# Modulation columns in the bank of their own products, and the group sums of the next step freed of waiting for them

## The chip, the cores and the metric
The kernel runs on one core of one Trainium2 chip. The metric is device time in microseconds (us) of one execution, the median of several runs. Before the change it is 2300.29 us (three runs, 2299.01 to 2300.86).

## What is computed
The reference is a two-layer backbone over 256 context and 256 latent tokens of width 1024. Layer 0 mixes tokens with a bidirectional Mamba-2 (SSD) mixer and then has a dense SwiGLU; layer 1 has windowed attention and a top-2-of-8 mixture of experts. Each layer is modulated by six vectors made of the condition. The change touches layer 0's mixer and its modulation alone. Cut to these, the reference is:

```python
mod_x = (silu(c) @ w_mod[i] + b_mod[i]).reshape(-1, 6, D_MODEL)        # and mod_c from c_ctx
hx = modulate(rmsnorm(x, norm1_w[i]), mod_x[:, 0], mod_x[:, 1])
...
def gated_rmsnorm(y, z, w):                                            # end of the SSD mixer
    g = (y * silu(z)).reshape(shp[:-1] + (SSD_GROUPS, D_INNER // SSD_GROUPS))
    g = g * rsqrt(mean(g * g, axis=-1, keepdims=True) + EPS)           # a mean over each group
    return g.reshape(shp) * w
...
out = gated_rmsnorm(y, z, norm_w) @ w_out
x = x + mod_x[:, 2][:, None] * yx
```

The mean square over each of the 8 groups (256 channels) is what "group sums", "group root", "group inverse" and "group spread" make below. The modulation vectors of layer 0 are made in 12 pairs of 512 columns; the first four are needed at once, the other eight (parts 2 to 5) only after the mixer, and they are made in the gaps of the group loop.

## The kernel before
**Layout.** Activations lie with channels on the partitions and the 512 tokens along the row. Weights come as units of 128 x 2048 numbers into a ring of four buffers; of each, ScalarE makes a high part (`dense_high`, L1211) and VectorE the rest (`dense_low`, L1608), and TensorE forms each product from three matmuls (`thrice`, L645, lines L647 to L649). Every engine's program is written out by hand, in the order in which it runs, and the engines wait for one another's semaphores with constants. The eight PSUM banks are `ps[0]` to `ps[7]`.

**The group loop.** TensorE's loop (L811) runs over g = 0 to 6; ScalarE's (L1366) and VectorE's (L1847) run alongside. In this document "pass g" is one turn of it. In pass g TensorE

1. at the head, if g > 0, makes the sums of group g-1 (`group_sums`, L698: 16 small matmuls into `ps[4]`, line L704);
2. does half of the x projection of group g+1 (24 matmuls of 512 columns, into `ps[0]` and `ps[1]`), then, if g > 0, `group_spread` (L708: 8 matmuls into `ps[5]`, line L713), which broadcasts the reciprocal roots, then the other half;
3. turns group g's tiles to tokens (`to_tokens`, L716: lines L723, L730 and L736, the last into `ps[5]`);
4. does the "bc" projection of group g+1, into `ps[0]` and `ps[1]` again, after it has waited for ScalarE's evacuation of x (`gemm_evac`, L820), with the chunk states (L744) in its middle;
5. makes one pair of modulation rows (`mod_pair`, L615, 32 matmuls of line L622, into `ps[5]`), the group's outputs (L766) and the z projection;
6. turns the modulation rows into columns (`turn_pair`, L626, 8 matmuls of line L631, into `ps[4]`), after VectorE has copied the rows out of `ps[5]` (`mod_rows`, L1640, line L1644).

VectorE, in pass g: the addition of bias to the columns of the pass before (`mod_out`, L1646, line L1655, which reads `ps[4]`), the reciprocal of the roots (`group_inverse`, L1748), a rest part, `finish` (L1757, which reads the spread), the token scales (`token_scales`, L1770), the decay tiles and the states, `mod_rows`, a rest part, one convolution (8 operations of L1742), the gating, a rest part and the second convolution. So `mod_out` stands behind the second convolution of the pass before. ScalarE, in pass g: z's evacuation (L1256), two Silus of the convolution (L1270), `group_root` (L1275, which reads the sums), a high part (L1219), 32 exponentials of segments (L1287), x's evacuation (L1248), the token tiles (L1297) and so on. Table loads stand between Silu, square root and exponential.

After the loop the last two groups follow, among the first parts of the output projection (`out_part`, L675), whose banks are 0 to 5.

Of the kernel before, what the change touches and what calls it, by code (L numbers as in the profile page):

```python
# [284 lines left out]
def backbone(nc, xt_in, vecs, wdt_in, bv_in, dense, experts_w, consts, out):  # L285
    es = ExitStack()
    with es:
# [7 lines left out]
        def sb(name, n, dt=F32):  # L295
            nonlocal top
            place_of[name] = top
            top += 4 * (n + (-n) % 8)
            assert top <= SB_BASE + 4 * SB_WORDS, (name, top)
            return at(name, place_of[name], n, dt)  # L300
# [13 lines left out]
        modT = sb("modT", 192)[:].rearrange("p (l m r) -> p l m r", l=2, m=48)  # L314
# [140 lines left out]
        ps = [es.enter_context(nc.psum_tensor(f"ps{i}", [P, 512], F32)) for i in range(8)]  # L455
# [14 lines left out]
        def vc(row, n=1):  # L470
            return col[:, row:row + n] if isinstance(row, int) else col[:, bass.ds(row, n)]


        S = {}
# [120 lines left out]
        def _(pe):  # L595
# [19 lines left out]
            def mod_pair(p, bank):  # L615

                for i in range(2):
                    n = D_AT[("m0", MOD_PAIRS[p][i], 0)]
                    pe.wait_ge(d_in[D_SLOT[n]], D_ARRIVED[n])
                    for k in range(KT):  # L620
                        c0 = 32 * (k % 4)
                        last = mm(ps[bank][c0:c0 + 32, 256 * i:256 * i + 256], csT[:, k, :],  # L622
                                  d_raw[D_SLOT[n]][:, 256 * k:256 * k + 256], start=k < 4, stop=k >= 4)
                    last.then_inc(S["d_used"], 1)

            def turn_pair(p, bank):  # L626

                pe.wait_ge(S["mrow_sb"], p + 1)
                for t in range(4):
                    a = 512 * (p % 2) + t * P  # L630
                    last = mm(ps[bank][:, 2 * t:2 * t + 2], mrow[:, a:a + P], rowsel, start=True, stop=True)  # L631
                last.then_inc(S["modt_ps"], 1)
# [42 lines left out]
            def out_part(j, h, ks):  # L675

                n = D_AT[("wout", j, h)]
                dense_wait(n)
                for k in ks:
                    pe.wait_ge(S["glo_done"], 1 + next(c for c, (a, w) in enumerate(G_CHUNKS) if a <= k < a + w))  # L680
                    top, low, _ = gate_parts(k, 1)
                    for t in range(2):
                        last = thrice(ps[OUT_BANK[2 * j + t]][:], dense_tile(n, k - 8 * h, t), (top, low), k == 0, k == 15)
                return last

            def gemm_part(kind, g, banks, ks):

                n = D_AT[(kind, g, 0)]
                dense_wait(n)
                for k in ks:  # L690
                    if g == 0:
                        pe.wait_ge(S["n_low"], k + 1)
                    for t in range(2):
                        last = thrice(ps[banks[t]][:], dense_tile(n, k, t), (h_top[:, k, :], h_low_[:, k, :]),
                                      k == 0, k == KT - 1)
                return last

            def group_sums(g):  # L698

                pe.wait_ge(S["ysq_done"], 2 * g + 2)  # L700
                pe.wait_ge(S["mod_done"], 5 + g)
                for t in range(2):
                    for c in range(NCH):
                        last = mm(ps[4][32 * c:32 * c + 32, 0:P], ones[:, 0:32], ysq[:, t, c * P:c * P + P],  # L704
                                  start=t == 0, stop=t == 1)
                last.then_inc(S["gsum_done"], 1)

            def group_spread(g):  # L708

                pe.wait_ge(S["grinv_done"], g + 1)  # L710
                for c in range(NCH):
                    pick = ident[:, 32 * c:32 * c + 1].to_broadcast([P, P])
                    last = mm(ps[5][:, c * P:c * P + P], pick, grs, start=True, stop=True)  # L713
                last.then_inc(S["gspread"], 1)

            def to_tokens(g):  # L716

                pe.wait_ge(S["cx_ready"], 4 * g + 4)
                pe.wait_ge(S["gemm_evac"], 6 * g + 6)
                for ch in range(NCH):  # L720
                    for t in range(2):
                        o = (ch % 2) * 256 + t * P
                        last = pe.transpose(ps[2 + ch // 2][:, o:o + P], cx[:, t, ch * P:ch * P + P], ident)  # L723
                    if ch % 2:
                        last.then_inc(S["tr_ready"], 1)
                if g == 0:
                    pe.wait_ge(S["ac_exp"], 1)
                    pe.wait_ge(S["ac_tail"], 1)
                for ch in range(NCH):
                    last = pe.transpose(ps[4][:, ch * P:ch * P + P], cx[:, 2, ch * P:ch * P + P], ident)  # L730
                last.then_inc(S["tr_ready"], 1)
                if g:
                    pe.wait_ge(S["gT_done"], 2 * g)
                for ch in range(NCH):
                    s = slice(ch * P, ch * P + P)
                    last = mm(ps[5][:, s], cx[:, 2, s], cx[:, 3, s], start=True, stop=True)  # L736
                last.then_inc(S["tr_ready"], 1)

            def states(g):

                pe.wait_ge(S["tok_evac"], 4 * g + 3)
                pe.wait_ge(S["xs_ready"], 2 * g + 2)
                for n, (d, ch) in enumerate(((0, 0), (0, 1), (0, 2), (1, 1), (1, 0), (1, 3))):
                    last = mm(ps[2 + n // 2][:, (n % 2) * 256:(n % 2) * 256 + 256], btok[:, ch, :], xtl[d][:, ch, :],  # L744
                              start=True, stop=True)
                last.then_inc(S["st_ready"], 1)
# [64 lines left out]
            for g in range(7):  # L811
                if g:
                    group_sums(g - 1)
                pe.wait_ge(S["gemm_evac"], 6 * g + 4)
                gemm_part("x", g + 1, (0, 1), range(4))
                if g:
                    group_spread(g - 1)
                gemm_part("x", g + 1, (0, 1), range(4, KT)).then_inc(S["d_used"], 1)
                to_tokens(g)
                pe.wait_ge(S["gemm_evac"], 6 * g + 8)  # L820
                gemm_part("bc", g + 1, (0, 1), range(4))
                states(g)
                gemm_part("bc", g + 1, (0, 1), range(4, KT)).then_inc(S["d_used"], 1)
                pe.wait_ge(S["tok_evac"], 4 * g + 4)
                mod_pair(4 + g, 5)
                if g == 0:
                    pe.wait_ge(S["ac_rows_sb"], 1)
                outputs(g)
                gemm_part("z", g + 1, (2, 3), range(KT)).then_inc(S["d_used"], 1)
                turn_pair(4 + g, 4)  # L830

            group_sums(6)
            group_spread(6)
            to_tokens(7)
            pe.wait_ge(S["gemm_evac"], 6 * 7 + 4)
# [1 line left out]
            states(7)  # L837
            pe.wait_ge(S["tok_evac"], 32)
            mod_pair(11, 5)
            pe.wait_ge(S["st_op"], 80)  # L840
            turn_pair(11, 4)
            out_part(1, 0, range(8)).then_inc(S["d_used"], 1)
            outputs(7)
            out_part(0, 1, range(8, 14))
            group_sums(7)
            out_part(1, 1, range(8, 14))
            group_spread(7)
# [733 lines left out]
        def _(dv):  # L1581
            TS, TT, STT = dv.tensor_scalar, dv.tensor_tensor, dv.scalar_tensor_tensor
# [63 lines left out]
            def mod_out(p):  # L1646

                dv.wait_ge(S["modt_ps"], p + 1)
                if p < 4:
                    dst = modT[:, 0, 0:16, :].rearrange("p (s k) r -> p s k r", s=2)[:, :, 2 * p:2 * p + 2, :]  # L1650
                    bias = vc(V_BMOD, 16).rearrange("p (s k) -> p s k", s=2)[:, :, 2 * p:2 * p + 2]
                    TT(dst, ps[3 + p % 2][:, 0:8].rearrange("p (s k r) -> p s k r", s=2, k=2),
                       bias.unsqueeze(3).to_broadcast([P, 2, 2, 2]), ALU.add).then_inc(S["mod_done"], 1)
                else:
                    TT(modT[:, 0, 4 * p:4 * p + 4, :], ps[4][:, 0:8].rearrange("p (m r) -> p m r", m=4),  # L1655
                       vc(V_BMOD + 4 * p, 4).unsqueeze(2).to_broadcast([P, 4, 2]), ALU.add).then_inc(S["mod_done"], 1)

            def first_alpha(p):
# [16 lines left out]
            for q in range(2):  # L1675
                r = slice(64 * q, 64 * q + 64)
# [366 lines left out]
            r = 0  # L2043
# [153 lines left out]
```

## Time and profile before

| | before |
|---|---|
| median of three runs | 2300.29 us (2299.01 to 2300.86) |
| the profiled execution's own time | 2299.07 us |
| its span, first to last instruction | 2297.3 us |
| mean granted TensorE clock | 0.964 |
| TensorE matmul busy | 2161.5 us |
| VectorE busy | 1495.1 us |
| ScalarE busy | 1236.9 us |
| bytes read from HBM | 504.45 MB, 221 GB/s over the span |

The span is what the profile's positions count in; the execution's own time is 1.8 us longer. The group loop lies between about 100 and 453 us of the span; the experts take the second half, in which the DMA engines are busy by 90% or more. A busy share is an average over stages with different limits. In the rows of time below, a number in brackets is the idle time of that engine before the instruction, and behind the arrow is what ended it; "PE" is TensorE, "DVE" VectorE, "ACT" ScalarE.

### The profile page before, as it was taken

The page shows a single profiled execution, that of the slowest core. Times are in us where ns is not written, and L with a number is a line of the kernel's source. Part 1 is how long each engine was busy: PE and PEld are TensorE (multiplying, and loading weights), DVE is VectorE, ACT ScalarE, POOL GpSimd, SP SyncE. Part 2 cuts the span into 40 slices and gives each one's busy share as a digit, 9 for nine tenths or more (in the row PEclk, how much of TensorE's full clock was granted, in tenths as well). Part 3 has the DMA queues.
Part 4 walks back from the last instruction along what each step waited for, and adds up shares of the span by engine and source line. Part 5 has one row for each costly group of instructions (what it writes and reads, how often), then busy time and mean ns, then how long its engine had stood idle before and what let it go on. Part 6 is the DMA issues. An engine that isn't in the chain of part 4 may idle for free.

```text
span 2297.3 us, 27395 instructions
## 1 busy us (share of the span) xinstructions
PE 2161.5 (94%) x11224; PEld 1729.8 (75%) x11224; DVE 1495.1 (65%) x1479; ACT 1236.9 (54%) x1394; POOL 45.7 (2%) x20
## 2 busy tenths in 40 slices
PE   6799999989899999988987999999999999999997
PEld 4678777767677777867566787887878787888875
DVE  3467777653332322245856887888878887888874
ACT  4566666642322222143545766676766666676763
POOL 0011111100000000000000000000000000000000
PEclk9899999979899999989997999999999999999998
DMA  8233454422244444325105999999999999999990
GB/s 301 94 129 129 148 185 173 173 94 74 87 170 165 166 169 155 107 74 175 48 1 193 345 344 356 330 364 334 342 340 342 339 338 350 336 362 333 344 344 21
DMA packets 137733, 509.61 MB, mean 222 GB/s; under 512 B 15296, under 2 KB 15680, under 8 KB 135296
## 3 DMA queue, kind: packets, MB, share of 16 engines
q1 hardware_dynamic: 137520, 507.65, 62.0%
q8 instruction: 90, 1.47, 0.3%
q14 instruction: 43, 0.35, 0.0%
q10 hardware_dynamic: 80, 0.13, 0.0%
HBM read 504.45 MB, written 3.28 MB: 221 GB/s over the span
## 4 chain that ended last, share of the span: by engine, by line
PE 83%; DVE 7%; ACT 4%; issue 1%; DVEq 0%; ACTq 0%
PE ps L1048 14%; PE ps L1046 14%; PE ps L1047 13%; PE ps L647 10%; PE ps L649 10%; PE ps L648 10%; DVE area L1742 3%; DVE d_lo L1613 2%; PE ps L957 1%; PE ps L975 1%; PE ps L1032 1%; PE ps L1105 1%; ACT area L1287 1%; PE ps L1075 1%; PE ps L659 1%
## 5 line engine op out<-in xcount | busy, mean ns | idle before, releaser
L2039 DVE TENSOR_TENSOR w_lo<-w_raw,w_hi 128x2048 fp32r<-128x2048 f32 x336 | 749.4, 2286 | 51.6 <-ACT w_hi L1496 50.7
L1496 ACT ACTIVATE w_hi<-w_raw 128x2048 fp32r<-128x2048 f32 x336 | 625.9, 1918 | 78.9 <-PE ps L1048 77.8
L1613 DVE TENSOR_TENSOR d_lo<-d_raw,d_hi 128x2048 fp32r<-128x2048 f32 (+1 forms) x76 | 171.9, 2262 | 334.4 <-ACT d_hi L1219 334.4
L1046 PE MATMUL ps<-w_hi,x_hi 128*128 128x512 f32 x896 | 357.1, 399 | 2.0 <-DVE x_lo L2095 2.0
L647 PE MATMUL ps<-h_top,d_hi 128*128 128x512 f32 (+1 forms) x816 | 331.5, 406 | 25.2 <-DVE h_low L1605 9.8
L1048 PE MATMUL ps<-w_hi,x_lo 128*128 128x512 f32 x896 | 355.0, 396 | 0.0
L1047 PE MATMUL ps<-w_lo,x_hi 128*128 128x512 f32 x896 | 350.7, 391 | 0.0
L1219 ACT ACTIVATE d_hi<-d_raw 128x2048 fp32r<-128x2048 f32 (+1 forms) x76 | 143.7, 1890 | 382.8 <-DMA d_raw<-in_dense 245.2
L649 PE MATMUL ps<-h_top,d_lo 128*128 128x512 f32 (+1 forms) x816 | 322.9, 396 | 0.0
L648 PE MATMUL ps<-h_low,d_hi 128*128 128x512 f32 (+1 forms) x816 | 319.1, 391 | 0.0
L647 PEld LDWEIGHTS ps<-h_top,d_hi 128*128 128x128 f32 x816 | 158.3, 194 | 69.6 <-issue 26.2
L1048 PEld LDWEIGHTS ps<-w_hi,x_lo 128*128 128x128 f32 x896 | 167.8, 187 | 41.6
L1047 PEld LDWEIGHTS ps<-w_lo,x_hi 128*128 128x128 f32 x896 | 168.5, 188 | 40.2
L1046 PEld LDWEIGHTS ps<-w_hi,x_hi 128*128 128x128 f32 x896 | 168.0, 187 | 39.2 <-DVE x_lo L2095 2.2
L649 PEld LDWEIGHTS ps<-h_top,d_lo 128*128 128x128 f32 x816 | 158.1, 194 | 35.7
L648 PEld LDWEIGHTS ps<-h_low,d_hi 128*128 128x128 f32 x816 | 158.9, 195 | 33.6
L1046 PE MATMUL ps<-w_hi,h_hi 128*128 128x512 f32 x448 | 179.9, 402 | 1.4 <-DVE h_lo L2111 1.4
L1048 PE MATMUL ps<-w_hi,h_lo 128*128 128x512 f32 x448 | 177.4, 396 | 0.0
L1047 PE MATMUL ps<-w_lo,h_hi 128*128 128x512 f32 x448 | 175.4, 392 | 0.0
L1048 PEld LDWEIGHTS ps<-w_hi,h_lo 128*128 128x128 f32 x448 | 83.9, 187 | 20.8
L1047 PEld LDWEIGHTS ps<-w_lo,h_hi 128*128 128x128 f32 x448 | 84.2, 188 | 19.9
L1046 PEld LDWEIGHTS ps<-w_hi,h_hi 128*128 128x128 f32 x448 | 84.0, 188 | 20.0 <-DVE h_lo L2111 1.7
(266 smaller groups left out, 2571.9 us busy)
## 6 DMA issues: line engine op xcount, KB each, us to landing
w_raw<-in_experts SPq DMA_DIRECT2D x672, 512.0 KB, 5.7
d_raw<-in_dense SPq DMA_DIRECT2D x240, 512.0 KB, 5.3
area<-acum_rows SPq DMA_DIRECT2D x16, 1024.0 KB, 8.4
d_raw<-in_dense SPq DMA_DIRECT2D x8, 384.0 KB, 4.2
xT<-in_xt SPq DMA_DIRECT2D x4, 512.0 KB, 6.7
gate_rows<-area SPq DMA_DIRECT2D x4, 512.0 KB, 6.7
hT<-gate_rows SPq DMA_DIRECT2D x2, 1024.0 KB, 6.0
cst<-in_consts SPq DMA_DIRECT2D x2, 512.0 KB, 11.2
```

The lines of the kernel that those rows point to most:

```text
L647: mm(o, w[0], v[0], start=first, stop=False)
L648: mm(o, w[0], v[1], start=False, stop=False)
L649: return mm(o, w[1], v[0], start=False, stop=last)
L659: last = mm(ps[6][c0:c0 + 32, 0:256], csT[:, k, :], d_raw[D_SLOT[n]][:, 256 * k:256 * k + 256], start=k < 4, stop=k >= 4)
L1046: mm(o, hi, w_hi[u % HIGH][:, a:a + 512], start=first, stop=False)
L1047: mm(o, hi, w_lo[u % RAW][:, a:a + 512], start=False, stop=False)
L1048: return mm(o, lo, w_hi[u % HIGH][:, a:a + 512], start=False, stop=last)
L1219: A(d_hi[si % D_HIGH][:, 0:w], d_raw[u][:, 0:w], ACT.Copy).then_inc(S["dhi_done"], 1)
L1496: A(w_hi[n % HIGH][:], w_raw[n % RAW][:], ACT.Copy).then_inc(S["whi_done"], 1)
L1613: TT(d_lo[u][:, 0:w], d_raw[u][:, 0:w], d_hi[si % D_HIGH][:, 0:w].bitcast(F32), ALU.subtract)\
L1742: STT(dst, raw[:, t, :, k:k + 256], vc(V_CW + 32 * k + conv_row(g, t)), dst, ALU.mult, ALU.add)\
L2039: TT(w_lo[n % RAW][:], w_raw[n % RAW][:], w_hi[n % HIGH][:].bitcast(F32), ALU.subtract)\
```

## The change
The turned columns of modulation pairs 4 to 11 are written into `ps[5]`, the bank in which their rows were made, and no longer into `ps[4]`; `mod_out` reads them there. `group_sums`, which writes `ps[4]`, no longer waits for `mod_out` (`mod_done`); `group_spread`, which writes `ps[5]`, now does, beside its wait for the reciprocal. The last turn loses its wait for the state operations of group 7 (`st_op`), which read `ps[4]`.

```diff
             def group_sums(g):
 
                 pe.wait_ge(S["ysq_done"], 2 * g + 2)
-                pe.wait_ge(S["mod_done"], 5 + g)
                 for t in range(2):
...
             def group_spread(g):
 
                 pe.wait_ge(S["grinv_done"], g + 1)
+                pe.wait_ge(S["mod_done"], 5 + g)
                 for c in range(NCH):
...
                 gemm_part("z", g + 1, (2, 3), range(KT)).then_inc(S["d_used"], 1)
-                turn_pair(4 + g, 4)
+                turn_pair(4 + g, 5)
...
             mod_pair(11, 5)
-            pe.wait_ge(S["st_op"], 80)
-            turn_pair(11, 4)
+            turn_pair(11, 5)
...
                 else:
-                    TT(modT[:, 0, 4 * p:4 * p + 4, :], ps[4][:, 0:8].rearrange("p (m r) -> p m r", m=4),
+                    TT(modT[:, 0, 4 * p:4 * p + 4, :], ps[5][:, 0:8].rearrange("p (m r) -> p m r", m=4),
                        vc(V_BMOD + 4 * p, 4).unsqueeze(2).to_broadcast([P, 4, 2]), ALU.add).then_inc(S["mod_done"], 1)
```

## Rows read from the trace of the kernel before

**Rows 1.** The page: busy time of the engines, and the chain that ended last.
```profile
PE 2161.5 (94%) x11224; PEld 1729.8 (75%) x11224; DVE 1495.1 (65%) x1479; ACT 1236.9 (54%) x1394; POOL 45.7 (2%) x20
...
PE 83%; DVE 7%; ACT 4%; issue 1%; DVEq 0%; ACTq 0%
```

**Rows 2.** Waits, 135 to 560 us: total us, times, longest us.
```profile
PE ps L704 <- DVE modT L1655: 9.2, 7, 1.5
...
PE ps L647 <- ACT area L1248: 1.3, 2, 0.7
```

**Rows 3.** Timeline, head of pass 2: start us, us, engine, line, operation.
```profile
200.60 0.95 PE L631 MATMUL ps<-cst 128*128 128x2 f32 x8
...
202.72 0.16 DVE L1655 TENSOR_TENSOR modT<-ps,col 128x8 f32<-128x8 f32 x1
...
203.02 0.65 PE L704 MATMUL ps<-area,cst 128*32 128x128 f32 x16 [1.47 <-DVE modT L1655]
...
205.18 0.95 DVE L1748 RECIPROCAL area<-area 128x128 f32<-128x128 f32 x1 [2.30 <-ACT area L1275]
...
210.82 1.05 PE L713 MATMUL ps<-area,cst 128*128 128x128 f32 x8
```

**Rows 4.** Timeline of ScalarE, pass 2.
```profile
202.17 1.29 ACT L1270 ACTIVATE area<-area 128x512 f32<-128x512 f32 x2 [0.29 <-DVE area L1742]
...
208.26 9.48 ACT L1287 ACTIVATE area<-area,atk 128x128 f32<-128x128 f32 x32
217.65 1.05 ACT L1248 ACTIVATE area<-ps 128x512 f32<-128x512 f32 x2
```

**Rows 5.** Timeline of VectorE, pass 2.
```profile
219.69 2.36 DVE L1770 TENSOR_TENSOR area<-area,tail 128x1024 f32<-128x1024 f32 x2 [6.37 <-ACT area L1297]
...
248.01 5.38 DVE L1742 SCALAR_TENSOR_TENSOR area<-area,col 128x512 f32<-128x512 f32 x8
```

**Rows 6.** Chain of waits in order of time: pass 1 (L1248) and pass 2 (L713).
```profile
167.78 0.97 ACT area L1248 x2
...
210.98 0.89 PE ps L713 x8
```

**Rows 7.** Timeline of VectorE: the copy of the modulation rows, passes 1, 2, 3, 5, 6.
```profile
184.71 0.69 DVE L1644 COPY cst<-ps 128x512 f32<-128x512 f32 x1 [0.18 <-PE ps L622]
...
235.30 0.69 DVE L1644 COPY cst<-ps 128x512 f32<-128x512 f32 x1 [0.81 <-PE ps L622]
...
285.92 0.69 DVE L1644 COPY cst<-ps 128x512 f32<-128x512 f32 x1 [0.84 <-PE ps L622]
...
386.40 0.69 DVE L1644 COPY cst<-ps 128x512 f32<-128x512 f32 x1 [0.73 <-PE ps L622]
...
437.01 0.69 DVE L1644 COPY cst<-ps 128x512 f32<-128x512 f32 x1 [0.83 <-PE ps L622]
```

**Rows 8.** Timeline of TensorE: first "bc" matmul of pass 1; last L736 of pass 2.
```profile
168.79 0.49 PE L647 MATMUL ps<-h_top,d_hi 128*128 128x512 f32 x1 [0.67 <-ACT area L1248]
...
218.59 1.06 PE L736 MATMUL ps<-area 128*128 128x128 f32 x8
```

**Rows 9.** Stretches: length, PE busy (count), granted clock, DMA share, GB/s.
```profile
168.80:172.20 3.40, 3.40 (x15) 1.00 0.44 175
203.67:210.80 7.13, 7.13 (x24) 0.76 0.21 82
304.88:310.40 5.52, 5.52 (x24) 1.00 0.27 106
...
355.28:361.90 6.62, 6.62 (x24) 0.83 0.17 71
```

**Rows 10.** Timeline of ScalarE behind the loop: the evacuation of the last z.
```profile
453.10 1.09 ACT L1256 ACTIVATE area<-ps 128x512 f32<-128x512 f32 x2 [4.83 <-PE ps L649]
```

**Rows 11.** Stretches in the router's part: transposes (L1011), and what follows them.
```profile
1227.95:1231.30 3.35, 3.35 (x18) 0.50 0.02 10
1231.40:1234.70 3.30, 0.99 (x9) 1.00 0.00 0
```

## The prediction
> **What bounds the kernel now.** I began with the shares on the page [rows 1]: TensorE is busy 94% of the span and carries 83% of the chain that ended last. That invites "every TensorE stall removed is time gained", but it is an average over stages, so I went on to the stage that is touched, the loop over the groups, some 400 us of 2297. I count by passes of that loop, 0 to 6; the sums of a group stand at the head of the pass after its own.
>
> The waits come next [rows 2]: `group_sums` (L704) sat 9.2 us in seven places for the addition that makes the modulation columns (L1655, VectorE): 1.5 us at the head of each of passes 1 to 6, and the little that is left behind the loop. In time order, at the head of pass 2 [rows 3]: the turning matmuls (L631) end at 200.60 + 0.95 = 201.55; the addition starts only at 202.72, because VectorE's queue holds a convolution ahead of it; TensorE idles 1.47 and starts the sums at 203.02. The group's reciprocal ends at 205.18 + 0.95 = 206.13, and the spread, which needs it, comes only at 210.82.
>
> Then the other engines, for what happens once TensorE is early. ScalarE [rows 4]: after the convolution's last Silu (202.17 + 1.29 = 203.46) it has no gap up to 218.70: square root, a high part, 9.48 us of segment exponentials from 208.26, and then the evacuation of the x projection (L1248, 217.65 to 218.70). The "bc" matmuls of TensorE write the same banks and wait for that evacuation. Behind it ScalarE reads the token tiles, for which VectorE had waited 6.37 us (L1770, 219.69) [rows 5]. From there VectorE is full up to the end of the pass's last convolution, 248.01 + 5.38 = 253.39, but for one hole: 0.81 us ahead of the copy of the modulation rows (L1644, in rows 7), which waits for the `mod_pair` matmuls behind "bc".
>
> So two loops of nearly one length run round each pass: one through VectorE and ScalarE (token scales, convolution, segments, evacuation), and TensorE's own. The chain of waits shows them change places [rows 6]: in passes 1 and 4 it runs through the evacuation L1248, in the others through TensorE's spread (L713). The hole ahead of L1644 tells the same [rows 7]: 0.18 us in pass 1 (and alike in pass 4), where the evacuation sets the pace; 0.81, 0.84, 0.73 and 0.83 in passes 2, 3, 5 and 6, where TensorE does. And where the evacuation does, TensorE waits for it already: 0.67 us at 168.79, the first "bc" matmul of pass 1 [rows 8].
>
> **The change, part by part.**
> 1. `group_sums` no longer waits for the addition. In pass 2 it may start at 201.6 instead of 203.0; its other condition, the squares, is met before ScalarE evacuates z. TensorE gains 1.5 us at this place, six times.
> 2. The wait moves to `group_spread`. The sums then end near 202.3, the 24 matmuls between take 5.5 us at the full clock [rows 9], so the spread is reached near 207.8. The addition is done at 202.9 and the reciprocal at 206.13: margins 4.9 and 1.7 us. The square root does not come earlier, as it stands behind the Silu that ends at 203.46. Cost 0, hidden by those 24 matmuls; without them the wait would stand here whole (behind the loop sums and spread follow each other, and nothing is gained).
> 3. The turn writes bank 5 instead of 4 and the addition reads it there: same instructions, same shapes, 0. The bank is free, since the turn already waits for its only reader, the copy L1644.
> 4. `turn_pair(11)` loses its wait for the state operations. VectorE copies the rows that it turns after those operations anyway: 0. No DMA moves and no queue's order changes, so SP's and POOL's queues stay as they are.
> 5. What is late next. In pass 2 the last small matmuls ahead of "bc" (L736) end at 218.59 + 1.06 = 219.65 [rows 8], after the evacuation's 218.70. Now they end near 218.2, so "bc" starts near 218.75, not 219.4: 0.65 us gained, and the other 0.8 turns into a wait. The hole ahead of L1644 falls from 0.81 to the 0.18 of the passes where the evacuation leads. In passes 1 and 4 nothing is gained: the wait of 0.67 grows to 2.15.
>
> The bounds of part 5: 0 if the freed time is lost entirely, 9.2 if all of it passes on. I take the value by the holes, which are the slack itself: (0.81 - 0.18) + (0.84 - 0.18) + (0.73 - 0.18) + (0.83 - 0.18) = 2.5 us. The last of the four passes on through the z matmuls, for which ScalarE waits 4.83 us at 453.10 [rows 10]. Everything after hangs on the loop's end and shifts as a whole.
>
> **The clock** is the unknown. After the sums of pass 2 the granted clock was 0.76 in the mean and the 24 matmuls took 7.13 us; in pass 5 they were 0.83 and 6.62; after those of pass 4, behind the same 1.5 us wait, 1.00 and 5.52 [rows 9]. A drop to 1.2 GHz costs 7.13 - 5.52 = 1.6 us, and now falls where part of it is slack. The change takes the wait from there and puts some 2.1 us ahead of "bc", behind transposes and small matmuls; a drop there delays L1644 and is paid whole. Bounds per pass: 0 and 1.6. I take 0, since behind the 0.67 us wait in the same place the clock stayed at 1.00 [rows 9], and keep 1.6 for the range: the new wait is three times as long.
>
> What transposes do for the clock decides here. From 1227.95 to 1231.30 TensorE did almost nothing but transposes, at 0.50, and right behind them the clock was 1.00 [rows 11]. The Trainium skill ("TensorE: Matmul & The Clock Gate", Part 4: PE-mode transpose) says that a transpose does not count as TensorE activity in the way other matmuls do. By that rule "bc" would start at the low clock in every pass, the result of rival C; the trace speaks against the rule.
>
> **Sum.** The profiled execution took 2299.07; 2299.07 - 2.5 = 2296.6. The median of the runs is 1.2 higher, 2300.29, and in its terms the forecast is **2297.8**. About 0.2% (4.6 us) is what a measurement can tell from no change.
>
> **Rivals.**
> A, the stall passes on whole: 2300.29 - 9.2 = 2291.1. For it: TensorE's 94% and its share of the chain. Against it: ScalarE's queue without a gap, and the 0.67 that TensorE waits already. It would need an earlier evacuation, and nothing brings that.
> B, the gain is given back: the low clock falls on "bc" in one or two of six passes, 1.6 each, which cancels 2.5: about 2300.3; three give 2302.6. For it: the clock fell in passes whose wait was 1.5 us. Against it: rows 11, and the 1.00 behind 168.79.
> C, slower: the low clock falls on "bc" in all six passes, as each has 2.1 us of waiting behind its transposes: 6 x 1.6 - 2.5 = +7.1, 2307.4. It passes 0.2% from five passes on (8.0 - 2.5 = 5.5). The same rows speak against it, more strongly, as every pass must fall.
> D, the change does not do what it says: the spread takes the wait over, no gain, 2300.3. For it only the thin margin of 1.7 us in part 2.
>
> **How the numbers follow.** Forecast 0.59, A 0.07, B 0.20, C 0.07, D 0.07. The range reaches up to three low-clock passes, 2302.6, and down to the forecast less the scatter of the runs (2299.01 to 2300.86) and a little of A, 2295.0; the rest of A and C are left out. Faster by over 0.2% is A and a little of the forecast, 0.09; slower is C, 0.07; within is the rest, 0.84.
>
> **What would show it.** Right: L704 waits for nothing, and neither does L713 in the loop; TensorE waits some 2.1 us for L1248 in all six passes; the hole before L1644 is 0.2 us everywhere; the chain runs through L1248 in each pass. Wrong by A: TensorE's waits for L1248 stay near 0.7. Wrong by B or C: a granted clock of 0.50 in the first "bc" matmuls, and holes before L1644 near 1.8. Wrong by D: waits at L713 of over 1 us. Holes gone and the time still lower than 2295 would show that I took a loop for closed that isn't.

## The result, and the profile after

The changed kernel takes **2305.74 us** (median of 9 runs, 2304.67 to 2307.52), against 2300.29 for the kernel before in the same comparison (9 runs, 2298.52 to 2301.93). The ratio is 1.0025, 95% interval 1.0016 to 1.0034: slower, by 5.5 us. The forecast was 2297.8 with a range up to 2302.6.

Line numbers from `group_sums` on are one lower than before: the sums are L703, the addition L1654, the copy of the rows L1643, the evacuation of x L1247, the token scales L1769. The profiled execution took 2306.15 us, its span is 2304.3 (before 2299.07 and 2297.3). The page answers rows 1 with this:

```profile
PE 2163.5 (94%) x11224; PEld 1730.9 (75%) x11224; DVE 1494.3 (65%) x1479; ACT 1236.7 (54%) x1394; POOL 45.6 (2%) x20
...
PE 80%; DVE 7%; ACT 6%; issue 1%; DVEq 0%; ACTq 0%
```

Nothing to see in the shares: 94% both times. Only the chain has moved, from TensorE (83% to 80%) to ScalarE (4% to 6%). The waits from 135 to 560 us, which answer [rows 2] (waiter, what it waited for, total us, times, longest us), say where to:

```profile
PE ps L647 <- ACT area L1247: 13.2, 6, 2.2
DVE cst L1643 <- PE ps L622: 11.7, 7, 2.7
PE ps L713 <- DVE area L1747: 3.5, 1, 3.5
```

The 9.2 us ahead of the sums are gone, with no line left of them. Instead TensorE waits 13.2 us in six places ahead of "bc", 2.2 each, where it had waited 1.3 in two. The spread waits only behind the loop, as it did. And VectorE's wait ahead of the copy of the modulation rows, 0.18 to 0.84 in passes 1 to 6 before [rows 7], is now this (VectorE's timeline: start, length, operation, and in brackets the idle time before it):

```profile
186.27 0.69 DVE L1643 COPY cst<-ps 128x512 f32<-128x512 f32 x1 [1.73 <-PE ps L622]
...
237.80 0.69 DVE L1643 COPY cst<-ps 128x512 f32<-128x512 f32 x1 [1.74 <-PE ps L622]
...
289.32 0.69 DVE L1643 COPY cst<-ps 128x512 f32<-128x512 f32 x1 [1.74 <-PE ps L622]
...
340.85 0.69 DVE L1643 COPY cst<-ps 128x512 f32<-128x512 f32 x1 [1.75 <-PE ps L622]
...
390.81 0.69 DVE L1643 COPY cst<-ps 128x512 f32<-128x512 f32 x1 [0.18 <-PE ps L622]
...
442.35 0.69 DVE L1643 COPY cst<-ps 128x512 f32<-128x512 f32 x1 [1.76 <-PE ps L622]
```

The gaps between these starts are 51.53, 51.52, 51.53, 49.96 and 51.54. A hole of 1.75 is 1.55 us too much, and five of the six passes have one; pass 5 alone has the hole of 0.18, and a copy 49.96 after the one before it, as I had forecast for all. What TensorE does at the head of "bc" in pass 2 and in pass 5, from its timeline:

```profile
220.32 0.51 PE L647 MATMUL ps<-h_top,d_hi 128*128 128x512 f32 x1 [2.21 <-ACT area L1247]
220.66 0.39 PE L648 MATMUL ps<-h_low,d_hi 128*128 128x512 f32 x1
220.89 0.53 PE L649 MATMUL ps<-h_top,d_lo 128*128 128x512 f32 x1
221.22 0.63 PE L647 MATMUL ps<-h_top,d_hi 128*128 128x512 f32 x1
...
374.89 0.50 PE L647 MATMUL ps<-h_top,d_hi 128*128 128x512 f32 x1 [2.20 <-ACT area L1247]
```

One matmul takes 0.39 us at first and 0.63 us within a microsecond of the restart. The granted clock, in stretches behind the start of "bc" in passes 1 to 6 (length, TensorE busy and number of matmuls, granted clock, DMA share, GB/s):

```profile
169.80:173.20 3.40, 3.40 (x9) 0.50 0.00 0
221.00:224.40 3.40, 3.40 (x10) 0.50 0.00 0
272.20:275.60 3.40, 3.40 (x10) 0.50 0.55 224
323.40:326.80 3.40, 3.40 (x8) 0.50 0.65 265
374.90:378.30 3.40, 3.40 (x15) 1.00 0.65 261
425.80:429.20 3.40, 3.40 (x10) 0.50 0.37 152
```

Half the clock (1.2 of 2.4 GHz) in the same five passes that have the hole of 1.75, full clock in pass 5, behind a wait of the same 2.20 us. While it lasts TensorE does 8 to 10 of these matmuls where it does 15 at full clock. After the sums, where the clock had fallen before [rows 9], it now stays up:

```profile
203.70:209.20 5.50, 5.50 (x24) 1.00 0.51 176
```

The loop's balance: 5 x 1.55 - 2.5 = +5.3. At the last turn of the loop, which starts at 458.24 and started at 452.90, the changed kernel is 5.34 behind. The medians differ by 5.45. The spans of the two profiled executions differ by 7.0; the other 1.7 us lie behind the loop. What lies outside the loop varies from one execution to the next: over the kernels of this study whose copy stands at its old place, the copy in pass 0 starts at 134.19 to 136.72, and from the copy in pass 6 to the end of the span it is 1858.5 to 1862.0 us. So a difference of a microsecond or two between medians is not read below as one of the loop; for the loop I take the distance from the copy in pass 0 to that in pass 6, which is 302.26 us before and 307.59 after.

### The profile page after: what moved, and what is told of

It is laid out like the page before. It is cut to its first block, busy times and chain, and to the rows that moved or that the text cites. A ratio compares the mean times of both kernels' runs of the same rounds, so it can differ in the third digit from the quotient of the medians.

```text
span 2304.3 us, 27394 instructions
## 1 busy us (share of the span) xinstructions
PE 2163.5 (94%) x11224; PEld 1730.9 (75%) x11224; DVE 1494.3 (65%) x1479; ACT 1236.7 (54%) x1394; POOL 45.6 (2%) x20
## 3 DMA queue, kind: packets, MB, share of 16 engines
q8 instruction: 90, 1.47, 0.3%
## 4 chain that ended last, share of the span: by engine, by line
PE 80%; DVE 7%; ACT 6%; issue 1%; DVEq 0%; ACTq 0%
PE ps L1047 14%; PE ps L1045 14%; PE ps L1046 13%; PE ps L647 9%; PE ps L649 9%; PE ps L648 9%; ACT area L1286 3%; DVE area L1741 3%; DVE d_lo L1612 2%; PE ps L956 1%; PE ps L974 1%; PE ps L1031 1%; PE ps L1104 1%; PE ps L1074 1%; PE ps L659 1%
```

## The experiments

My theory after the result: the new 2.2 us wait ahead of "bc" brings the low clock, "bc" is on VectorE's path through the `mod_pair` matmuls, and each such pass pays 1.55 us. Rivals: the bank change costs it; the clock is a symptom only; any wait of TensorE costs; the loss is in the stage behind the loop. All edits are to the changed kernel, except where it says otherwise; each comparison has 11 runs of the kernel and 27 to 33 of the kernel before, on the same chip. The changed kernel itself was not measured again in them, so a difference to its 2305.74 is one between comparisons; the median of the kernel before was 2299.84 to 2300.29 in all of them.

### The bank alone

```diff
                 pe.wait_ge(S["ysq_done"], 2 * g + 2)
+                pe.wait_ge(S["mod_done"], 5 + g)
...
                 pe.wait_ge(S["grinv_done"], g + 1)
-                pe.wait_ge(S["mod_done"], 5 + g)
```

> The changed kernel with the wait for the modulation columns put back ahead of the group sums; only the bank of the turned columns stays changed. Theory (the moved TensorE wait brings the low clock onto the bc matmuls, 1.55 us in each of five passes, less the 2.5 gained): as before, 2300.3, TensorE waits 1.5 us at the sums and at most 0.7 ahead of bc, and the hole ahead of the copy of the modulation rows (L1643 here) is 0.2 to 0.8. Rival 1 (the bank costs it: the turned columns in bank 5 delay something): 2305.7 stays. Rival 2 (a chance of placement in the program): somewhere between, with the same waits as before.

Measured: 2300.58 us, ratio 1.0001 (0.9992 to 1.0010). The waits:

```profile
PE ps L704 <- DVE modT L1654: 9.2, 7, 1.5
...
PE ps L647 <- ACT area L1247: 1.3, 2, 0.7
```

These are the waits of before to the digit, and the loop is 302.29 us. The passes in which TensorE waits for the evacuation are now 2 and 6, and were 1 and 4: with the same waits the clock falls behind the sums in four passes of six again, but not in the same four. The bank costs nothing; the loss comes with the moved wait.

### The new wait filled with work

```diff
                 to_tokens(g)
+                if g:
+                    for _ in range(8):
+                        mm(ps[6][:], h_top[:, 0, 0:P], h_top[:, 0, :], start=True, stop=True)
                 pe.wait_ge(S["gemm_evac"], 6 * g + 8)
```

> The changed kernel with eight matmuls of 512 columns, whose result nobody reads, between the token tiles and the wait for the x evacuation in passes 1 to 6: TensorE waits as before but does not idle. Theory: eight take 1.8 us of the 2.1 of waiting, the granted clock stays at 1.00 in the bc matmuls, the hole ahead of the copy falls from 1.7 to 0.2, and the time to 2305.7 - 5 x 1.55 = 2298 (2297.8 as forecast). Rival (the clock is a symptom, and bc starts late for another reason): no gain, 2305.7, or more, as eight matmuls are added. Rival 2 (the tail behind the loop holds the loss, 1.7 us of it by the spans): 2299.5.

Measured: 2296.92 us, ratio 0.9987 (0.9978 to 0.9996). TensorE now does 48 matmuls more, and the kernel is 8.8 us faster than without them. The loop is 299.87 us, 7.7 less than in the changed kernel. Pass 2 from the timeline, and the clock of passes 1 and 2 (stretches as above):

```profile
218.03 2.10 PE L822 MATMUL ps<-h_top 128*128 128x512 f32 x8
220.49 0.51 PE L647 MATMUL ps<-h_top,d_hi 128*128 128x512 f32 x1 [0.36 <-ACT area L1250]
```

```profile
170.40:173.80 3.40, 3.30 (x14) 1.00 0.04 17
220.40:223.80 3.40, 3.31 (x14) 1.00 0.05 18
```

"bc" still starts when the evacuation lets it; only the clock differs, and it is 1.00 behind that start in all six passes. They are 49.97 to 49.99 us long, the holes ahead of the copy 0.18 to 0.19. The clock is the cause, not a symptom: the price of five low passes, 5 x 1.55, is what the loop has lost in length. The rival that put 1.7 us behind the loop forecast 2299.5, above all 11 runs (2295.45 to 2299.10).

### The old wait filled with work, in the kernel before

```diff
                 if g:
+                    for _ in range(6):
+                        mm(ps[5][:], h_top[:, 0, 0:P], h_top[:, 0, :], start=True, stop=True)
                     group_sums(g - 1)
```

> The kernel before, unchanged but for six matmuls of 512 columns, whose result nobody reads, in its wait of 1.5 us ahead of the group sums in passes 1 to 6. Theory: the low clock after the sums (four of six passes) was what cost the kernel before its 0.65 us in each of four passes; with it gone the evacuation leads in every pass, the holes are 0.2, and the time is 2300.3 - 2.5 = 2297.8. Rival (the lost 0.65 came of the wait itself, 1.5 us of TensorE's loop): the wait is as long as it was, so nothing changes, 2300.3.

Measured: 2296.02 us, ratio 0.9984 (0.9975 to 0.9993). The wait ahead of the sums is used up, TensorE waits for the evacuation in all six passes:

```profile
PE ps L647 <- ACT area L1250: 4.0, 6, 0.7
...
PE ps L704 <- DVE modT L1657: 0.4, 1, 0.4
```

The clock no longer falls behind the sums; it is 1.00 there in all six passes, in pass 2:

```profile
203.50:206.90 3.40, 3.40 (x29) 1.00 0.65 229
```

The loop is 299.82 us, 2.44 less than in the kernel before. So the 2.5 us that the change was to bring could be had without it. The medians differ by 4.0; the rest is outside the loop, and what it is isn't shown. What the kernel before lost at this place was not the 1.5 us of waiting, which is still spent, but the low clock behind it. This is also the fastest version of the study by its median, though three others lie within 1 us of it, less than their runs scatter.

### A wait added

```diff
             def group_spread(g):
 
                 pe.wait_ge(S["grinv_done"], g + 1)
                 pe.wait_ge(S["mod_done"], 5 + g)
+                if g < 6:
+                    pe.wait_ge(S["dlo_done"], 3 * g + 8)
```

> The changed kernel with one more wait ahead of the group spread in passes 1 to 6, for the rest part of the bc weights (ready some 1.5 us later than TensorE gets there). It adds a wait and no work. Theory: the 2.1 us of waiting split into 1.5 in the middle of the x projection and 0.6 ahead of bc; bc stays at full clock, and a drop behind the spread falls where there is slack: 2298 to 2300.5, faster than the changed kernel by 5 or more although a wait is added. Rival (any further wait of TensorE can only cost): 2305.7 or more.

Measured: 2297.04 us, ratio 0.9983 (0.9974 to 0.9992): 8.7 us faster than the changed kernel by a wait and nothing else. The spread now waits, and the clock stays up around it and in "bc" (stretches of pass 2: ahead of the spread, up to and over most of its wait, behind the wait, behind the start of "bc"):

```profile
211.40 1.13 PE L715 MATMUL ps<-area,cst 128*128 128x128 f32 x8 [1.54 <-DVE d_lo L1614]
```

```profile
204.00:207.40 3.40, 3.40 (x19) 1.00 0.83 296
207.50:210.90 3.40, 2.36 (x11) 1.00 0.00 0
211.40:214.80 3.40, 3.40 (x19) 1.00 0.00 0
220.70:224.10 3.40, 3.37 (x15) 1.00 0.53 211
```

The same 2 us of idle time per pass, cut into 1.54 in the midst of dense matmuls and 0.4 ahead of "bc", cost nothing: the clock is 1.00 behind both waits in all six passes. That the length of a wait is not all is to be seen here too. The kernel before waited 1.47 us between its small turning matmuls and the small matmuls of the sums, and lost the clock in four passes of six; 1.54 us between matmuls of 512 columns lost it in none.

### How long a wait does it take

The same filler, with four, two and one matmuls:

```diff
-                    for _ in range(8):
+                    for _ in range(4):
```

> As the kernel with eight unread matmuls ahead of the x evacuation's wait, with four (0.9 us), so that 1.2 of the 2.1 us of waiting remain. Theory: the kernel before waited 1.5 at the sums and lost the clock in four passes of six, and 0.67 ahead of bc with no loss; 1.2 lies between, nearer to safe as matmuls stand on both sides: clock at 1.00 in bc in at least five of six passes, 2297 to 2299. Rival (only a wait that is filled nearly whole is safe): 2300 to 2305.7 with several low stretches.

> Two unread matmuls of 512 columns ahead of the x evacuation's wait in passes 1 to 6: 0.46 us filled, 1.75 of waiting left. Waits of 1.28 (four matmuls) lost nothing, of 1.9 one or two passes of six by the times, of 2.2 nearly all. Theory (it is the length of the wait that brings the low clock): 0 or 1 low passes, 2297 to 2298.5. Rival (a lock: a low pass of 51.5 us brings the next, whatever the length): as with one matmul, either none or nearly all.

> One unread matmul: 0.23 us filled, some 1.97 of waiting left. Theory (length of the wait): some passes low, 2298.5 to 2303, between the kernels with two matmuls and with none. Rival (the lock): near 2305 if one pass falls at all; or 2297.

| matmuls of filler | wait left ahead of "bc" | median us | ratio to before (95%) |
|---|---|---|---|
| 8 | 0.4 | 2296.92 | 0.9987 (0.9978 to 0.9996) |
| 4 | 1.3 | 2296.29 | 0.9986 (0.9977 to 0.9995) |
| 2 | 1.7 | 2297.58 | 0.9989 (0.9980 to 0.9998) |
| 1 | 2.0 | 2304.13 | 1.0019 (1.0010 to 1.0028) |
| 0 | 2.2 | 2305.74 | 1.0025 (1.0016 to 1.0034) |

The waits left are from the views of the waits (with two, and with one):

```profile
PE ps L647 <- ACT area L1250: 10.4, 6, 1.7
```

```profile
PE ps L647 <- ACT area L1250: 11.8, 6, 2.0
```

With four and with two matmuls the clock is 1.00 in all six passes, and the holes are 0.17 to 0.19. One matmul of a quarter of a microsecond decides over 6.5 us of the median, and over 7.8 us of the loop (299.78 with two, 307.60 with one). I had expected something in between for one matmul. The loop with one is as long as with none (307.59), so the 1.6 us between these two medians are not the loop's. With one matmul the profile shows the same passes low as with none, 1 to 4 and 6, with 5 spared:

```profile
325.00:328.40 3.40, 3.40 (x9) 0.51 0.60 245
376.40:379.80 3.40, 3.40 (x15) 1.00 0.63 255
427.40:430.80 3.40, 3.40 (x10) 0.51 0.33 135
```

### Transposes as filler

```diff
-                    for _ in range(8):
-                        mm(ps[6][:], h_top[:, 0, 0:P], h_top[:, 0, :], start=True, stop=True)
+                    for q in range(12):
+                        o = slice(q % 4 * P, q % 4 * P + P)
+                        pe.transpose(ps[6][:, o], cx[:, 2, o], ident)
```

> Twelve transposes of 128 columns, whose result nobody reads, in the place of the eight matmuls, some 1.5 us: of the 2.2 of waiting 0.7 is left, and transposes and small matmuls alone fill the place ahead of bc. Theory (transposes keep the clock as other matmuls do; the row in the router's part says so): no low clock in bc, as with eight matmuls, 2297. Rival (they do not count, as a page of the skill has it): the clock drops in every pass as with no filler or more, 2305.7 to 2307.

Measured: 2297.13 us, ratio 0.9989 (0.9980 to 0.9998). The stretch ahead of "bc" in pass 2, and the clock behind it:

```profile
215.85 1.47 PE L823 MATMUL ps<-cst,area 128*128 128x128 f32 x12
218.22 0.50 PE L647 MATMUL ps<-h_top,d_hi 128*128 128x512 f32 x1 [0.90 <-ACT area L1251]
```

```profile
218.20:221.60 3.40, 3.38 (x15) 1.00 0.03 11
```

The time without other matmuls is as long as in the changed kernel, 1.47 + 0.90, and the clock holds. If transposes did not count, this would have been a gap longer than the 2.2 that lost it. The page of the Trainium skill that the prediction weighed ("TensorE: Matmul & The Clock Gate", Part 4: PE-mode transpose) says that a transpose does not count as TensorE activity in the way other matmuls do; for these transposes of 128x128 f32 that is not borne out by this run, in which the clock is 1.00 behind all six waits.

### Three passes of six

```diff
-                if g:
+                if g % 2:
                     for _ in range(8):
```

> The eight unread matmuls in passes 1, 3 and 5 alone. Theory (each pass pays its own low clock, 1.55): passes 1, 3 and 5 at 50.0 us, those of 2, 4 and 6 that drop at 51.5; if all three drop 2297 + 3 x 1.55 = 2301.7. In the changed kernel four drops in a row were followed by one pass without; if a drop makes that of the next pass likelier, because the pass is then 51.5 and not 50.0 long, fewer than three of 2, 4 and 6 drop here: 2297 to 2300. Rival (the loss is one of the loop's start or end, not of the passes): 2297 or 2305.7, no value between.

Measured: 2300.74 us, ratio 1.0000 (0.9991 to 1.0009), 3.8 above the kernel with the filler in all six. The profiled execution (2300.77) had one low pass in the loop, pass 4, and that one pass is 1.55 longer:

```profile
286.18 0.69 DVE L1646 COPY cst<-ps 128x512 f32<-128x512 f32 x1 [0.18 <-PE ps L622]
337.71 0.69 DVE L1646 COPY cst<-ps 128x512 f32<-128x512 f32 x1 [1.74 <-PE ps L622]
387.67 0.69 DVE L1646 COPY cst<-ps 128x512 f32<-128x512 f32 x1 [0.18 <-PE ps L622]
```

The price is paid in the pass that has the low clock, so the rival "start or end of the loop" falls. But the time of this kernel is not a count of low passes: its loop is 301.35 us, 1.5 more than with the filler in all six, and from the copy in pass 6 to the end it takes 2.2 more (1861.35 against 1859.18). What lengthens that part isn't shown.

The three passes without filler have the wait of the changed kernel, and the clock fell in one of them (first "bc" matmul of passes 2, 4 and 6, and stretches behind it):

```profile
220.30 0.50 PE L647 MATMUL ps<-h_top,d_hi 128*128 128x512 f32 x1 [2.19 <-ACT area L1250]
...
320.24 0.50 PE L647 MATMUL ps<-h_top,d_hi 128*128 128x512 f32 x1 [2.21 <-ACT area L1250]
...
421.72 0.51 PE L647 MATMUL ps<-h_top,d_hi 128*128 128x512 f32 x1 [2.21 <-ACT area L1250]
```

```profile
220.30:223.70 3.40, 3.40 (x15) 1.00 0.02 10
321.40:324.80 3.40, 3.40 (x10) 0.51 0.29 117
421.80:425.20 3.40, 3.40 (x15) 1.00 0.63 257
```

So a wait of 2.2 us can cost the clock and need not: it did in five passes of six of the changed kernel, and in one of three here.

### The copy taken off VectorE's path

```diff
-                mod_rows(4 + g)
                 dense_low(3 * g + 5)
                 convolve(g + 1, 0)
+                mod_rows(4 + g)
```

> The changed kernel with VectorE's copy of the modulation rows moved behind the rest part and the first convolution (7.6 us later), so that VectorE no longer stands at it when the mod_pair matmuls are late. No work is added. Theory 1 (the low clock in bc costs the loop through that copy alone): passes fall to 49.8 us although the clock still drops, the holes ahead of the copy are 0, time near 2297. Theory 2 (the delay of 1.55 runs on through outputs and the z matmuls to ScalarE's evacuation of z, which has under 1 us of slack ahead of the convolution's Silus): passes of about 51 us, some 0.4 less than the 51.5 of the changed kernel, time about 2303.5. I expect theory 2. Rival (the low clock is harmless): 2305.7.

Measured: 2298.10 us, ratio 0.9990 (0.9981 to 0.9999), far below both 2303.5 and 2305.7. The wait ahead of "bc" is shorter than in the changed kernel, 11.0 us in six places against 13.2: 1.67 and 1.66 in passes 1 and 4, 1.92 to 1.93 in the other four, which is between the waits left by two filler matmuls and by one. The clock fell in two of these four, 3 and 6; passes 3 and 5 have the same wait:

```profile
269.06 0.49 PE L647 MATMUL ps<-h_top,d_hi 128*128 128x512 f32 x1 [1.93 <-ACT area L1247]
...
369.73 0.50 PE L647 MATMUL ps<-h_top,d_hi 128*128 128x512 f32 x1 [1.93 <-ACT area L1247]
```

The clock in passes 3 and 6:

```profile
270.30:273.70 3.40, 3.40 (x9) 0.50 0.37 149
420.50:423.90 3.40, 3.40 (x10) 0.50 0.42 172
```

Passes without it are 49.69 us, and pass 3, with it, 50.99 (the token scales start at 270.00 and 320.99). So theory 2 is right on the price: 1.30 of the 1.55 us come through even with VectorE not waiting, by the z matmuls and ScalarE's evacuation of z. Its time was wrong because the number of low passes changed, which neither theory had: the later copy also shortened the wait.

Both edits together, the filler and the later copy:

> Eight unread matmuls in passes 1 to 6 and the copy of the modulation rows moved behind the first convolution. Theory: with the clock kept, the last holes of 0.18 us go as well, 49.8 us a pass: 1 us below the kernel with the eight alone, near 2296. Rival (TensorE's z matmuls then set the pace through ScalarE's evacuation): no difference, 2297.

Measured: 2296.56 us, ratio 0.9985 (0.9976 to 0.9994), passes of 49.69. The last holes of 0.18 and a little more are gone, and the median is 0.4 below the filler's alone, which can't be told from none.

## Why the prediction was wrong

It failed at one step, "The clock": "Bounds per pass: 0 and 1.6. I take 0, since behind the 0.67 us wait in the same place the clock stayed at 1.00". It was 1.55 in five of the six passes of the profiled execution. I had written next to it that the new wait is three times as long, and took the near row for the place and not for the length. The nearest row by length was the other one, the wait of 1.5 us ahead of the sums, behind which the clock had fallen in four passes of six. The two rows don't bracket 2.2; both lie below it. At this place the profiled executions show no drop behind waits of up to 1.75 us, and drops behind some, not all, of those from 1.92 us on.

A second wrong turn is in the use of rows 11. That transposes hold the clock up is right (the transposes as filler show it), and I let it speak against a drop. But that row has no wait in it like the new one, and with nothing in the wait the clock fell in five passes of six. What the prediction set beside rival C, that the transposes ahead of the wait do not count, is not what the runs show either; its condition, a wait of over 2 us in each pass, is what came, and five passes of six fell.

The rest held in its sizes, term by term. Part 1: the wait at the sums is gone. Part 2: no wait at the spread in the loop. Parts 3 and 4: the bank alone is 1.0001. Part 5: TensorE waits 2.2 in each pass (2.15 forecast), the hole is 0.18 in the pass whose clock stayed, and that pass is 49.96 long.

One reason in part 5 is not as I gave it. For pass 2 it leaves 0.8 us of wait; the 2.2 measured there needs also that the clock no longer falls behind the sums (24 matmuls in 5.50 us, 7.13 before). And the filler in the kernel before brings the 2.4 us with its wait still spent, so that kernel has the gain without the early start that part 5 puts it down to. The 2.5 us are there when the clock is held: the loop is 299.87 with eight matmuls, 2.4 less than before. The median, 2296.9 against the 2297.8 of the forecast, is lower by more than the loop gives.

What came is rival C, at the point where it begins to decide: five passes, for which it gave 8.0 - 2.5 = +5.5, and 5.45 was measured. It had 0.07, which was far too little beside a row of 1.5 us of waiting that had lost the clock in four passes of six; the range should have reached its 2307.4.

Rival A is refuted by its own sign: TensorE's waits for the evacuation are 2.2 us and not 0.7, and with the clock held the passes stay at 49.97. In the list of signs, "a granted clock of 0.50 in the first bc matmuls, and holes before L1644 near 1.8" is what the profile shows.

**What stays open** is which of several equal waits loses the clock. In the changed kernel it falls in four passes in a row, and then not behind the very same wait; with one filler matmul (1.97 us of wait) the same five passes are low; with the filler in every other pass one wait of 2.2 in three loses it, and with the later copy two of 1.93 in four. A drop that lengthens its pass (51.52 us instead of 49.97) so that the next falls in the same way would fit the four in a row. It doesn't explain the fifth, and the drop in pass 4 of the kernel with every other pass filled came behind passes of full clock. No run here holds the wait and varies the length of the pass alone, and each kernel has one profiled execution.

## What to carry to other kernels

Moving a stall of TensorE from one place to another is not neutral even when it grows by nothing on the whole: whether the clock falls behind a gap depends here on how long the single gap is and on what stands around it (1.7 us ahead of "bc" and 1.54 among dense matmuls lost nothing, 1.47 among small matmuls lost four passes of six), and the price is paid where the slow matmuls stand: 0.65 us a pass behind the sums, 1.55 in "bc". Before a short wait is merged with another, compare the sum of the two with the gaps in the trace behind which the clock fell; and look at who waits for the matmuls that would then run slow. Where a gap could not be avoided here, it cost less cut in two, or filled with matmuls that nobody reads, than in one piece.

## What I had not expected

A step this sharp in the time: 1.7 us of idle time ahead of "bc" cost nothing measurable, 2.0 us cost 6.5 us in all. For a single pass it is no rule, as waits of 1.9 and 2.2 us went both ways. That added work and an added wait both made the kernel faster by nearly 9 us, the 48 matmuls to 2296.92 and the wait to 2297.04. And that the kernel before had the same loss in a milder form: 2.4 us of its loop come back when its old wait is filled (2296.02, ratio 0.9984).
